# The weight stream with five raw buffers in place of seven

## The reference

```python
mod = c_act @ w_ada[l] + b_ada[l]                     # 6 x 1024 scales, shifts and gates
h = modulate(rms_norm(x, norm_mix[l]), sh1, sc1)
p = h @ w_in[l]                                       # attention, rwkv, gmlp and gate columns
y_att, y_rwkv, y_gmlp = attention(p), rwkv7_time_mix(p), chunked_spatial_gating(p)
x = x + gt1 * ((gates * branch).sum() @ w_out[l])
h = modulate(rms_norm(x, norm_ffn[l]), sh2, sc2)
x = x + gt2 * conv_gated_ffn(h, ...)                  # up 1024 -> 2 x 2816, down 2816 -> 1024

h = x + 0.5 * swiglu(rms_norm(x), w_ffn1_in[i], w_ffn1_out[i])
h = h + (g_attn * window_attention(...) + g_conv * depthwise_conv(...)) @ w_o[i]
h = h + 0.5 * swiglu(rms_norm(h), w_ffn2_in[i], w_ffn2_out[i])
x = h + (p[i] @ w_pe_proj[i]) * sigmoid(rms_norm(h) @ w_pe_gate[i])
```

## Time and profile before

| | |
|---|---|
| time, median of 3 runs | 2216.38 us (2216.26 to 2217.41) |
| profiled execution, span from the first to the last instruction | 2213.9 us |
| busy PE, DVE, ACT | 99%, 76%, 57% |
| DMA moved | 415.15 MB, mean 188 GB/s |
| weight blocks loaded, ACT splits, DVE splits | 664, 656, 656 |
| modulation blocks loaded after the first 16 | 80 |
| granted TensorE clock, mean | 0.996 |

### The profile page before, as it was taken

How to read it: one execution, slowest core, us unless ns; L and a number is a source line. 1 busy time by engine, 2 the same in 40 slices (tenths; PEclk the granted TensorE clock), 3 DMA queues, 4 the chain that set the end, 5 groups by cost and what they waited for, 6 DMA issues and landing times.

```text
span 2213.9 us, 39422 instructions
## 1 busy us (share of the span) xinstructions
PE 2184.1 (99%) x16412; PEld 1988.8 (90%) x16412; DVE 1677.7 (76%) x2609; ACT 1266.3 (57%) x2098; POOL 12.5 (1%) x20
## 2 busy tenths in 40 slices
PE   7999999999999999999999999999999999999999
PEld 6898989998999888999888899988898889998888
DVE  7777568987885648877687678788678866878875
ACT  4755446554756446555556457665565555676554
POOL 0000000000000000000000000000000000000000
PEclk9999999999999999999999999999999999999999
DMA  9454555777745347655555543565555554346554
GB/s 375 169 173 164 167 189 198 268 242 261 249 153 182 115 154 227 220 172 187 179 190 189 189 134 115 172 209 190 186 177 190 190 190 144 114 162 202 190 189 133
DMA packets 116228, 415.15 MB, mean 188 GB/s; under 512 B 13089, under 2 KB 16289, under 8 KB 115538
## 3 DMA queue, kind: packets, MB, share of 16 engines
q1 hardware_dynamic: 116050, 412.63, 55.9%
HBM read 409.42 MB, written 3.16 MB: 186 GB/s over the span
## 4 chain that ended last, share of the span: by engine, by line
PE 93%; DVE 3%; ACT 2%; DMA 1%; issue 0%; SPq 0%; ACTq 0%; DVEq 0%
PE bank L198 93%; DVE arena L205 1%; DMA raw<-W 1%; ACT arena L250 1%; PE bank L202 1%; DVE lo L205 1%; DVE arena L213 0%; ACT hi L250 0%; DMA xT<-x 0%; ACT L250 0%; ACT L242 0%; DVE h L205 0%; DVE ada L222 0%; SPq L195 0%; DVE y1l L205 0%
## 5 line engine op out<-in xcount | busy, mean ns | idle before, releaser
L198 PE MATMUL bank<-h,hi 128*128 128x256 f32 (+1 forms) x5344 | 1226.8, 315 | 0.0
L250 ACT ACTIVATE hi<-raw 128x1024 fp32r<-128x1024 f32 x656 | 689.1, 1056 | 598.5 <-PE bank L198 551.7
L198 PE MATMUL bank<-h,lo 128*128 128x256 f32 x3440 | 989.3, 288 | 5.6 <-DVE h L205 5.3
L198 PEld LDWEIGHTS bank<-h,hi 128*128 128x128 f32 x5344 | 883.4, 191 | 67.1 <-issue 2.6
L205 DVE TENSOR_TENSOR lo<-raw,hi 128x1024 fp32r<-128x1024 f32 x656 | 794.6, 1222 | 92.2 <-ACT hi L250 91.0
L198 PEld LDWEIGHTS bank<-h,lo 128*128 128x128 f32 x3440 | 656.7, 191 | 17.9 <-DVE h L205 6.8
L198 PE MATMUL bank<-act,hi 128*128 128x512 f32 x1056 | 370.0, 393 | 0.0
L198 PE MATMUL bank<-act,lo 128*128 128x256 f32 x1056 | 294.7, 279 | 0.0
L198 PEld LDWEIGHTS bank<-act,hi 128*128 128x128 f32 x1056 | 197.9, 187 | 47.1
L198 PE MATMUL bank<-arena 64*64 64x64 f32 (+8 forms) x2994 | 221.8, 262 | 6.3 <-DVE arena L205 3.2
L198 PEld LDWEIGHTS bank<-arena 64*64 64x64 f32 (+3 forms) x2994 | 170.7, 146 | 39.4 <-issue 9.4
(11 more groups left out here) (150 smaller groups left out, 1911.8 us busy)
## 6 DMA issues: line engine op xcount, KB each, us to landing
raw<-W SPq DMA_DIRECT2D x664, 512.0 KB, 3.4
ada<-WA SPq DMA_DIRECT2D x80, 512.0 KB, 3.9
arena<-WA SPq DMA_DIRECT2D x16, 512.0 KB, 14.6
p_projected<-arena SPq DMA_DIRECT2D x2, 1024.0 KB, 7.8
arena<-scr SPq DMA_DIRECT2D x16, 128.0 KB, 4.7
arena<-p_projected SPq DMA_DIRECT2D x2, 1024.0 KB, 5.0
xT<-x SPq DMA_DIRECT2D x2, 512.0 KB, 5.3
arena<-lora SPq DMA_DIRECT2D x2, 512.0 KB, 10.5
```

The source lines that it names most:

```text
L198: return self.done(lambda e: e.matmul(out, l, r, start=start, stop=stop, skip_group_check=True))
L250: return self.done(lambda e: e.activation(out, in_, f, scale=scale, **kw))
```

## The change

`RAW` goes from seven to five. The raw buffers that share their memory with `lo` become five, as many as the `hi` buffers, and so do the semaphores of their landings. The load of block b now waits for PE's block b - 5 in place of b - 7, and SP's `at_block(b)` issues the load of block b + 5 in place of b + 7. At the start SP issues five weight blocks between the first modulation blocks in place of seven (`if k < RAW`). Everything placed behind the buffers in SBUF moves down by 8 KB, and the arena at the end grows by as much; no tile in it changes its size or place within the arena. The number of DMAs, instructions and bytes stays the same.

```diff
@@ -30,7 +30,7 @@
 NABLK = L * 48
 PAR0 = 78
 CB = BT * 128
-RAW, HL, RAWA = 7, 5, 2
+RAW, HL, RAWA = 5, 5, 2
 U0 = 16512
 KB = 1024
```

## The result

| | before | five raw buffers |
|---|---|---|
| median of 4 runs each, same chip | 2216.32 us (2216.17 to 2217.41) | 2535.86 us (2525.44 to 2537.70) |
| ratio, 95% interval | | 1.1433 [1.1418, 1.1447] |
| profiled span | 2213.9 us | 2535.2 us |
| granted TensorE clock, mean | 0.996 | 0.957 |
| time at the lower of its two levels (1.2 GHz) | 17 us | 220 us |

A forecast was written before the change was run, and what follows sets the result against it. PE, busy 99% of the span, was taken as the bound. Terms of 78 + 50 + 22 + 5 = 155 us on the 2213.9 us span gave 2369, with 2.5 us for the median 2371, stated as 2370; range 2280 to 2455.

The forecast's parts named there:

- The modulation ring: Up and down projections: modulation, SP's load, splits and a later modulation wait on each other in a circle; 78 us.
- I count none there: Recurrences: ticks take 4 to 5 us, two ticks exceed the ring's 8.4, so no ring cost.
- The steps of the side chains: Recurrences, merges, group norms, attentions: ACT's result copies come late behind a waiting split; 50 us, bounds 20 to 90.
- the changes of phase: About twelve places where a projection's last eviction stands behind a split, up to 3.3 us each; 22 us.
- the start: Start of the kernel: blocks 13 and 14 are issued behind the small tables; 5 us (0 to 12).
- ACT stands for a landing at its splits: ACT's waits for PE at splits become waits for landings, several hundred, over 1000 us.
- Plain feed-forward stretches lose nothing: Feed-forward stretches without modulations: slack of 8.6 us covers the 3.3 us shift; blocks stay at 2.88 us.
- The ring in the up projections: Both layers' up projections: modulations 12.0 us apart where PE wants 8.64; 19 x 3.4 = 65 us.
- End of down and the way to the next layer: End of the down projection: modulations two blocks apart, ring 8.4 against 5.8 us; 2.6 x 3 = 8 us.
- The second, 2490: Rival: the ring binds in the recurrences too, and side steps pay landings of 4.3 to 5 us; 2490, chance 0.17.
- Latency only: Rival: the modulation ring does not close, only the other terms' 77 us remain; 2293, chance 0.2.
- not slower: Rival: all of the 3.3 us shift is covered by slack; 2214 to 2218, chance 0.03.

The follow-up runs named there:

- experiment 1: Changed kernel with the modulation ring cut: four ada buffers, SP waiting for the modulation two back; 2390.27 us, 1.0790 of the kernel before.
- the four kernels: The changed kernel, then it with the ring cut, with ACT's and DVE's splits one block later, with both: 2535.86, 2390.27, 2272.48, 2236.93 us.
- the experiment made for it: Changed kernel with six extra 128x128x128 matmuls on constants ahead of PE's waits in 56 recurrence steps; 2575.78 us, 1.1615 of the kernel before.
- experiment 9: Changed kernel with only ACT's split one block later in its queue, DVE's as it was; 2469.55 us, 1.1143 of the kernel before.

## Why the prediction was right or wrong

The sum of 155 us fell 165 short, in two terms. The modulation ring was put at 78 us and is worth 146 (cutting it gives that back): the step that failed is "I count none there" for the recurrences, together with ending the ring at the down projection. The steps of the side chains, the changes of phase and the start were put at 77 us and are worth 174 with the ring cut: there the step that failed is the discount, 18 us for all attentions and half of the changes of phase taken as covered. This parting cuts the ring first, as the prediction adds its terms; cut last, with the splits already late, the ring is worth 36. The lower clock, which had no term, lies inside both.

- **ACT stands for a landing at its splits: right.** 1011.3 us and 452 waits at 656 splits, "several hundred, over 1000 us" had been said. The reason is shown: seven buffers with the rule of five are as slow, six and six as well.
- **Plain feed-forward stretches lose nothing: right.** 123.5 us in both, and at most 1.7 us in 32 blocks elsewhere.
- **The ring in the up projections: right in place and size.** 12.5 us a turn against 12.0 forecast. Cutting the ring gives back 49 us in the first layer's up stretch and 15 in blocks 222 to 332: 64, where 65 was forecast. Part of the landings was worse than assumed (median 5.4 us in this stretch, 4.4 before).
- **"I count none there", the ring in the recurrences: a step that failed.** The cut gives back 19 and 30 us there, 50 in all. Ticks of 4 to 5 us had been set against a closed ring of 8.4, from one modulation to the next. The chain of the changed kernel does not need a closed ring: nine times in the two recurrences it goes from a modulation to SP's issue, to a landing of 4.1 to 6.9 us, to ACT's split and from there to a side step's copy or a norm's small operation, for which PE stands in the end (298.51 to 305.93 in the second piece of chain below). Only once, from 1042.57 to 1053.89, does it come straight back to the next modulation. With the ring cut it never goes through SP there. So the late load costs through ACT's queue wherever a side step stands behind the split. That this path carries all of the 50 us is argued from the chain, not shown.
- **End of down and the way to the next layer: 8 counted, 25 measured** (103.4 to 78.2). Down itself 16 for 11. The forecast ended the ring with the down projection; the chain of the changed kernel goes around it through the norms and the next layer's first blocks:

```profile
672.50 1.20 DVE ada L222
...
673.73 0.33 SPq L195
...
674.58 6.54 DMA raw<-W
...
681.15 1.06 ACT hi L250
...
682.24 1.22 DVE lo L205
683.46 1.19 DVE ada L222
```

  One turn is 10.96 us, with a landing of 6.54. The ring's term thus was 78 and measures 155 by stages (64 + 50 + 25 + 16). The medians give 146: the profiled run of the kernel with the ring cut was the fastest of its four, and from block 332 on it was 4 us longer.
- **Steps of the side chains and changes of phase: 77 with the start, 174 measured** (2390.27 less 2216). In the two recurrences the size was near: 28 + 3 + 13 = 44 forecast, 22.8 + 23.2 = 46 measured with the ring cut. But PE ran there 29 us more at the lower clock than before, at 0.44 up to 13 us of the 46, which the sum did not have; so part of the agreement is luck. The chain of the changed kernel shows the steps, three landings in 25 us:

```profile
298.51 1.19 DVE ada L222
299.74 0.33 SPq L195
...
300.11 4.10 DMA raw<-W
304.24 0.29 ACT hi L250
...
305.20 0.59 ACT arena L250
...
305.93 4.23 PE bank L198 x56
...
310.17 4.07 DMA raw<-W
...
314.27 1.06 ACT hi L250
315.32 0.49 ACT arena L250
...
315.86 4.22 PE bank L198 x56
...
320.10 3.31 DMA raw<-W
```

  The second block was mis-sized: 88 us (at 0.44, up to 22 of them the clock), of which its two mixers (attention and convolution) are 47 (blocks 354 to 398 and 542 to 586 took 165.7 each and take 189.4 and 188.5 with the ring cut), while all four attentions had been given 18 and all changes of phase 22. A chain of small ACT operations behind each split pays a landing per tick, as the chain of experiment 1 shows: from the landing at 1460.12 until PE goes on at 1472.94 it passes 3.4 us of landing and then 9.4 us of ACT's split and small operations. The start measured 14 for 5, and the stages between the recurrences and up to block 332 another 21; the rest up to 174 is the 5 us by which the profiled run lay under the median.
- **The clock: not seen at all.** 203 us more at the lower level. At 0.44 that is at most 89 us of the 320; it is less, since in a ring the clock's loss is partly hidden: in the up projection three blocks need 8.64 us plus 3 (0.44 of 6.8, the usual piece there), still under 12.5. Of the four kernels, time at the lower clock falls as PE's waits do (220, 111, 46, 24 us), so it is counted here as a part of the two terms and not as a third cause. How much of each it is, stays open; the experiment made for it failed.
- **The rivals.** The second, 2490, was nearest, and right that the modulations cost time in the recurrences (80 us said, 50 measured) and that side steps are dearer. Its reason for the latter, landings of 4.3 to 5 us, holds for a part of those on the chain (3.2 to 6.9 us in the recurrences), while the median there is 3.3 to 3.4; the second block, with no modulations and landings of 3.3 and 3.4 us on the chain shown, lost the most. So side steps were dearer mainly because more of them paid. Its chance of 0.17 was too small, because both its parts follow from the same standing queues. Latency only is refuted by SP's waits and by experiment 1, "not slower" by the time. The double-buffering rule of the Trainium skill ("Trainium Kernel Development and Optimization", Best Practices), read as in the prediction, would call five or six raw buffers as ample as seven. No run here agrees: six raw and five `hi` cost 2.3%, six and six 14.3%, five and five 14.3%; in the plain stretches alone the rule holds.

## What to carry to other kernels

A buffer's count is not its lead: where a load waits for the same event as the instruction that will consume it, the consumer's in-order queue stands for a whole landing each time, and everything behind pays; take the consumer one step later in its queue before buying buffers, and whoever waits for the consumer with it (experiment 9). Look in the DMA-issuing queue for waits on another stream's work of the same step, for they turn a lead of two steps into a ring. And where the bound engine stops being the bound, count its lower clock as a cost of the waits, for at 1.2 GHz the matmuls here lost 0.42 to 0.44 of their time.

## What was not expected of the hardware

- TensorE's clock went to 1.2 GHz in 41 pieces of 3.4 to 13.7 us, 220 us in all. In the up projection of the first layer, 44 us of them, PE was busy 148.6 of 180 us, with waits like the one of 5.11 us above; before, busy without a gap, the same stretch had none.
  The windows of that stretch, after and before:

```profile
421.00:601.00 180.00, 148.55 (x1085) 145.72 (x1084) 111.28 (x179) 65.93 (x109) 0.00 (x0) 0.89 0.48 172
```
```profile
358.00:486.00 128.00, 128.00 (x1069) 128.00 (x1068) 115.97 (x192) 71.74 (x118) 0.00 (x0) 1.00 0.73 250
```

- Landings in the ring got slower with fewer buffers, though over the whole kernel they did not: median 5.4 and at most 10.0 us in the up stretch, against 4.4 and 6.2, at 172 GB/s for 250. There the modulation block and three weight blocks are issued within 1.8 us (525.01 to 526.76), where before three weight blocks alone took 5.52. That the burst is the reason is argued only.
